# Sums of squares by token quarters on 32 partitions each, root and reciprocal on 128 columns

## The reference

```python
def layer_norm(x, g, b):
    x32 = x.astype(jnp.float32)
    mu = jnp.mean(x32, axis=-1, keepdims=True)
    var = jnp.mean(jnp.square(x32 - mu), axis=-1, keepdims=True)
    y = (x32 - mu) * lax.rsqrt(var + LN_EPS)
    return (y * g.astype(jnp.float32) + b.astype(jnp.float32)).astype(x.dtype)

def rms_norm(x, g):
    x32 = x.astype(jnp.float32)
    y = x32 * lax.rsqrt(jnp.mean(jnp.square(x32), axis=-1, keepdims=True) + RMS_EPS)
    return (y * g.astype(jnp.float32)).astype(x.dtype)
...
    a = jax.nn.silu(layer_norm(a, ln_a_g, ln_a_b))          # branch a, width 512
...
    for i in range(DEPTH):                                   # second block
        h = rmsnorm(x, norm_g[i]) * (1.0 + sc[:, None, :]) + sh[:, None, :]
...
    return rmsnorm(x, norm_f)
```

## Time and profile before

| | |
|---|---|
| Time, median of 3 runs | 2353.86 us |
| Lowest and highest run | 2351.16 and 2355.52 us |
| Profiled execution, span of its instructions (its whole time is not given apart) | 2352.3 us |
| TensorE busy | 2254.0 us, 96% |
| VectorE busy | 1487.5 us, 63% |
| ScalarE busy | 850.4 us, 36% |
| GpSimd busy | 1082.5 us, 46% |
| Mean granted TensorE clock, as a share of 2.4 GHz | 0.988 |

### The profile page before, as it was taken

How to read it: one execution, slowest core, us unless ns; L and a number is a source line. 1 busy time by engine, 2 the same in 40 slices (tenths; PEclk the granted TensorE clock), 3 DMA queues, 4 the chain that set the end, 5 groups by cost and what they waited for, 6 DMA issues and landing times.

```text
span 2352.3 us, 29969 instructions
## 1 busy us (share of the span) xinstructions
PE 2254.0 (96%) x10766; PEld 1834.4 (78%) x10766; DVE 1487.5 (63%) x2357; ACT 850.4 (36%) x1387; POOL 1082.5 (46%) x1273
## 2 busy tenths in 40 slices
PE   6899999999999999999999999999999999999997
PEld 3688777788668877788867888887877878788886
DVE  5989866554478986765368776555775766533322
ACT  2443334222353333422245434344343444433321
POOL 1565436565446543666534455341444344443343
PEclk9999999999999999999999999999999999999999
DMA  8432224664243221354322223233244242222222
GB/s 307 134 110 82 68 73 143 207 202 156 72 143 108 81 67 59 130 169 149 116 81 73 92 99 104 79 116 119 85 123 138 90 126 77 71 72 72 72 81 72
DMA packets 93204, 259.80 MB, mean 110 GB/s; under 512 B 10129, under 2 KB 11537, under 8 KB 92945
## 3 DMA queue, kind: packets, MB, share of 16 engines
q1 hardware_dynamic: 71392, 210.23, 28.6%
q10 hardware_dynamic: 21680, 47.79, 5.7%
HBM read 237.01 MB, written 20.97 MB: 110 GB/s over the span
## 4 chain that ended last, share of the span: by engine, by line
PE 41%; issue 29%; POOL 19%; DVE 7%; ACT 2%; DMA 1%; POOLq 0%; ACTq 0%; DVEq 0%; SPq 0%
POOL t L422 19%; PE bank L2132 13%; PE bank L2133 13%; PE bank L2134 13%; DVE t L1786 3%; PE bank L2206 1%; DVE t L1224 1%; PE bank L2183 1%; DMA t<-blocks 1%; PE bank L2522 1%; DVE t L1228 0%; PE bank L2225 0%; DVE t L1783 0%; POOL t L432 0%; DVE t L1257 0%
## 5 line engine op out<-in xcount | busy, mean ns | idle before, releaser
L422 POOL TENSOR_TENSOR t<-t,t 128x256 fp32r<-128x256 f32 x1208 | 1030.5, 884 | 1179.4 <-ACT t L485 1178.9
L2132 PE MATMUL bank<-t,t 128*128 128x512 f32 (+1 forms) x3056 | 1175.4, 385 | 32.9 <-DVE t L1224 9.4
L2133 PE MATMUL bank<-t,t 128*128 128x512 f32 (+1 forms) x3056 | 1148.4, 376 | 0.0
L2134 PE MATMUL bank<-t,t 128*128 128x512 f32 (+1 forms) x3056 | 1147.2, 375 | 0.0
L2132 PEld LDWEIGHTS bank<-t,t 128*128 128x128 f32 x3056 | 580.0, 190 | 163.5 <-issue 16.0
L2133 PEld LDWEIGHTS bank<-t,t 128*128 128x128 f32 x3056 | 580.0, 190 | 103.2 <-issue 4.2
L2134 PEld LDWEIGHTS bank<-t,t 128*128 128x128 f32 x3056 | 578.4, 189 | 105.1
L485 ACT ACTIVATE t<-t 128x1024 fp32r<-128x1024 f32 x302 | 317.2, 1054 | 287.5 <-PE bank L2134 240.1
L1288 DVE SCALAR_TENSOR_TENSOR t<-t,t,t 128x512 f32<-128x512 f32 x168 | 156.4, 950 | 101.8 <-DMA t<-w_ada 62.0
L1571 DVE SCALAR_TENSOR_TENSOR t<-t,t,t 128x512 f32<-128x512 f32 x240 | 206.1, 859 | 6.7
L1228 DVE SCALAR_TENSOR_TENSOR t<-t,bank 128x512 f32<-128x512 f32 x112 | 76.7, 685 | 153.3 <-ACT t L1181 59.9
(11 more groups left out here) (251 smaller groups left out, 1731.2 us busy)
## 6 DMA issues: line engine op xcount, KB each, us to landing
t<-blocks SPq DMA_DIRECT2D x306, 512.0 KB, 3.6
t<-w_ada SPq DMA_DIRECT2D x144, 256.0 KB, 2.7
t<-w_ada SPq DMA_DIRECT2D x20, 512.0 KB, 11.6
xm_park<-t ACTq DMA_DIRECT2D x16, 384.0 KB, 2.3
s_park<-t ACTq DMA_DIRECT2D x16, 384.0 KB, 2.3
t<-xm_park ACTq DMA_DIRECT2D x16, 384.0 KB, 4.5
t<-s_park ACTq DMA_DIRECT2D x16, 384.0 KB, 5.0
xc_park<-t ACTq DMA_DIRECT2D x16, 256.0 KB, 2.3
```

The lines of the kernel that those rows point to most:

```text
L422: low = pool.tensor_tensor(w_lo[slot][:, part], w_raw[slot][:, part], w_hi[slot][:, part].bitcast(F32), ALU.subtract)
L2132: pe.matmul(out, wh, xh, start=start, stop=False)
L2133: pe.matmul(out, wh, xl, start=False, stop=False)
L2134: return pe.matmul(out, wl, xh, start=False, stop=stop)
```

## The change

The norms named above sum, root and invert in another layout. The 512 tokens are cut into four quarters of 128. For each tile of squares TensorE now issues four products instead of one (`sum_quarters`): each takes 32 columns of ones and 128 tokens, and writes 32 partitions of the bank, quarter j on partitions 32j to 32j + 31. The sums are then 128 x 128, and ScalarE's root and VectorE's reciprocal work on 128 columns. `spread` brings the result back to 128 x 512: four products of 128 columns, whose stationary operand is one column of the identity matrix repeated 128 times, which picks row 32j. It writes a PSUM bank, and VectorE scales the tiles with that bank instead of `tmp[2]`.

TensorE's queue gets the spreads at fixed places, each with a wait for VectorE's reciprocal: in the middle of a chunk (`middle`) for the q norms, for branch a (in `merge(0, 1)`) and for the layer norm of layer 1 (in the first context tile), and between fillers for the other layer norm, `n0` and `n1`, where seven fillers become one, the spread, and two. The last norm's spread ends TensorE's program. The sum of the keys and values' squares waits in addition for the scaled q latents (`qn`), since both use bank 2. The wait of the first context tile for the root `x_std` is gone.

```diff
             def norm_std(cols, n, label, tmp=tmp, bank=3):
                 act.wait_ge(pe_done, P(*label, "sq", n - 1))
+                if cols == S:
+                    cols = S // 4
                 act.activation(tmp[2][:, 0:cols], banks[bank][:, 0:cols], ACT.Sqrt, bias=eps_rms[:], scale=1.0 / (128 * n))\
...
-                act.activation(tmp[2][:], banks[3][:], ACT.Sqrt, bias=eps_x[:], scale=1.0 / D).then_inc(act_done, a(l, "x_std"))
+                act.activation(tmp[2][:, 0:128], banks[3][:, 0:128], ACT.Sqrt, bias=eps_x[:], scale=1.0 / D).then_inc(act_done, a(l, "x_std"))
...
             def norm_recip(cols, label, tmp=tmp):
                 wa(*label, "std")
+                if cols == S:
+                    dve.reciprocal(tmp[2][:, 0:S // 4], tmp[2][:, 0:S // 4]).then_inc(dve_done, d(*label, "rstd"))
+                    wp(*label, "spread")
+                    return
...
             def x_norm(l, j):
-                dve.scalar_tensor_tensor(x[:, j, :], x[:, j, :], V("ln_g", l, j), tmp[2][:], ALU.mult, ALU.mult).then_inc(dve_done, d(l, "x_norm", j))
+                dve.scalar_tensor_tensor(x[:, j, :], x[:, j, :], V("ln_g", l, j), banks[6][:], ALU.mult, ALU.mult).then_inc(dve_done, d(l, "x_norm", j))
...
                 wa(l, "x_std")
-                dve.reciprocal(tmp[2][:], tmp[2][:]).then_inc(dve_done, d())
-                wd()
-                wd()
+                dve.reciprocal(tmp[2][:, 0:128], tmp[2][:, 0:128]).then_inc(dve_done, d(l, "x", "rstd"))
+                wp(l, "x", "spread")
...
+            def sum_quarters(bank, tile, first, last, label):
+
+
+                for j in range(4):
+                    mm = pe.matmul(bank[32 * j:32 * j + 32, 0:128], ones[:, 0:32], tile[:, 128 * j:128 * (j + 1)], start=first, stop=last)
+                mm.then_inc(pe_done, p(*label))
+
+            def spread(bank, quarters, label):
+
+
+                pe.wait_ge(dve_done, Dn(*label, "rstd"))
+                for j in range(4):
+                    row = ident[:, 32 * j:32 * j + 1].to_broadcast([128, 128])
+                    mm = pe.matmul(bank[:, 128 * j:128 * (j + 1)], row, quarters[:, 0:128], start=True, stop=True)
+                mm.then_inc(pe_done, p(*label, "spread"))
...
-                    keep_busy(5, 7)
+                    keep_busy(5, 1)
+                    spread(banks[6], tmp[2], (l - 1, "x"))
+                    keep_busy(5, 2)
...
-                    sum_rows(banks[2], tmp[j % 2][:], 3, j, (l, "q_sq", j))
+                    sum_quarters(banks[2], tmp[j % 2], j == 0, j == 2, (l, "q_sq", j))
                 pe.wait_ge(act_done, A(l, "q_lat", 0))
-                u_chunk(banks[0], B_KVL(l) + 1, (l, "kv_lat", 1))
+                turn = lambda: spread(banks[2], tmp[2], (l, "q"))
+                u_chunk(banks[0], B_KVL(l) + 1, (l, "kv_lat", 1), turn if l else None)
...
-                u_chunk(banks[1], B_KR(l), (l, "k_rope"))
+                u_chunk(banks[1], B_KR(l), (l, "k_rope"), None if l else turn)
...
                     pe.wait_ge(act_done, A(l, "kv_lat_sq", j))
+                    if j == 0:
+                        pe.wait_ge(dve_done, Dn(l, "qn", 2))
...
-                    sum_rows(banks[3], tmp[j % 2][:], NA, j, (l, "a_sq", j))
-                merge(0, 1)
+                    sum_quarters(banks[3], tmp[j % 2], j == 0, j == NA - 1, (l, "a_sq", j))
+                merge(0, 1, lambda: spread(banks[3], tmp[2], (l, "a")))
...
-            pe.wait_ge(act_done, A(L1 - 1, "x_std"))
-            context_tile(0)
+            context_tile(0, lambda: spread(banks[6], tmp[2], (L1 - 1, "x")))
             context_tile(1)
             norm_sums(range(KT), S, ("n0",), sq_t, 5)
-            keep_busy(7, 7)
+            keep_busy(7, 1)
+            spread(banks[5], tmp[2], ("n0",))
+            keep_busy(7, 2)
...
             sums_of_two(("nf",), f_sum, f_s[(KT - 1) % 2])
+            spread(banks[3], f_rstd, ("nf",))
```

More of the change, by code:

```diff
@@ L1754, in _ @@
             norm_recip(S, ("n0",))
-            norm_parts(x, uH, uL, range(KT), S, lambda j: ada[:, 2, j:j + 1], ("n0",), ready=lambda j: (L1 - 1, "y", j))
+            norm_parts(x, uH, uL, range(KT), S, lambda j: ada[:, 2, j:j + 1], ("n0",), ready=lambda j: (L1 - 1, "y", j), rstd=banks[5])
             def xm_parts(h, c):
@@ L2063, in _ @@
             norm_recip(S, ("n1",))
-            norm_parts(x, uH, uL, range(KT), S, lambda j: ada[:, 4, j:j + 1], ("n1",))
+            norm_parts(x, uH, uL, range(KT), S, lambda j: ada[:, 4, j:j + 1], ("n1",), rstd=banks[3])
             def fu_parts(g):
@@ L2138, in w_at, with chunk @@
                 return h[:, s * 128:(s + 1) * 128], lo[:, s * 128:(s + 1) * 128]
-            def chunk(out, tiles, label, ends=()):
+            def chunk(out, tiles, label, ends=(), middle=None):
                 for n, (b, s, xh, xl) in enumerate(tiles):
+                    if n == len(tiles) // 2 and middle:
+                        middle()
                     if n == 0 or b != tiles[n - 1][0]:
@@ L2153, in chunk, with u_chunk @@
                     pair_columns(b)
-            def u_chunk(bank, b, label):
-                chunk(bank[:], [(b, k, uH[:, k, :], uL[:, k, :]) for k in range(KT)], label, (b,))
+            def u_chunk(bank, b, label, middle=None):
+                chunk(bank[:], [(b, k, uH[:, k, :], uL[:, k, :]) for k in range(KT)], label, (b,), middle)
             def first_chunks(out, b, labels, ready, xh=uH, xl=uL, middle=None):
@@ L2218, in context_tile @@
                 for k in range(KT):
+                    if k == KT // 2 and middle:
+                        middle()
                     product(banks[2 + c][:, 0:CTX], *w_at(b, k), cH2[:, k, :], cL2[:, k, :], k == 0, k == KT - 1)
@@ L2223, in norm_sums @@
                     pe.wait_ge(act_done, A(*label, "sq", j))
-                    tile = sq_t[j % 3] if tmp is sq_t else tmp[j % 2]
+                    if tmp is sq_t:
+                        sum_quarters(banks[bank], sq_t[j % 3], j == 0, j == KT - 1, (*label, "sq", j))
+                        continue
+                    tile = tmp[j % 2]
                     pe.matmul(banks[bank][:, 0:cols], ones[:], tile[:, 0:cols], start=(j == 0), stop=(j == KT - 1))\
@@ L2439, in _, with merge @@
                         turn_outputs(3)
-                def merge(jj, k):
+                def merge(jj, k, middle=None):
                     n = 3 * jj + k
@@ L2772, in _ @@
             sums_of_two(("n1",), tmp[3], sq_t[(KT - 1) % 3])
-            keep_busy(7, 7)
+            keep_busy(7, 1)
+            spread(banks[3], tmp[2], ("n1",))
+            keep_busy(7, 2)
             def fu(g):
```

40 lines of the change are left out of this document (19 added, 21 removed).

## The result

The changed kernel took 2341.55 us (median of 4 executions, 2338.44 to 2344.25), beside 2352.99 of the kernel before on the same chip. The ratio is 0.9948 with a 95% interval of 0.9931 to 0.9964. That is 12.2 us less than before by the ratio (11.4 by the medians), where 14.1 less, to 2339.8, were forecast. The mean of the four is 0.9946, or 12.8 us.

The account below looks back on a forecast made before the run. TensorE, busy for 96% of the span, was taken as the bound. Gains of 3.87, 5.5, 4.6 and 3.6 us sum to 17.6; less 3.5 for the clock, 14.1 from 2353.9 gives 2339.8 us, range 2335 to 2349.

Parts of the forecast that it names:

- The fixed part per norm: Every changed norm: shorter reciprocal saves 2.40 us, shorter root 0.33, spread costs 1.15; gain 1.58 us.
- Quarters side by side: Sums on TensorE: four quarter products in different column groups overlap, holding TensorE 0.25 us instead of 0.87.
- rival B: Sums: quarters run one after another, 0.88 us a sum; only 5.7 us gained, 2348.2 us; chance 0.17.
- Rival C: Sums: each change of column group drains TensorE, 1.24 us a sum; slower, 2359.7 us; chance 0.08.
- Place 1: End of layer 0: root starts 2.29 us earlier, and with the fixed 1.58 the gain is 3.87 us.
- Place 2: End of layer 1 and the norm behind it: first scaled tile starts at 1232.85 instead of 1238.34, 5.5 us gained.
- Place 3: Norm before the Fourier layer and the last norm: 2.3 us gained each, together 4.6.
- Branch a: Norm of branch a: shorter sums, and the 1.30 us wait behind it goes; 1.8 us a layer, 3.6 together.
- The q norms: q norms of both layers: shorter sums and the spread's cost, bounded by -0.4 and +0.9 a layer; taken as 0.
- The clock: Sparser TensorE work brings 1.2 GHz stretches; five places at 0.7 take back 3.5 us, bounds 0 and 8.5.
- Rival A: Clock falls over bound work in all five places, taking 8.5 us; 9.1 us gained, 2344.8 us; chance 0.20.
- The sum: Whole kernel: place gains total 17.6 us, less 3.5 for the clock, so 14.1 us gained.

Follow-up runs that it names:

- The mean of the four: Mean over four timed groups of the changed kernel, unedited, each beside the kernel before: ratios 0.9948, 0.9941, 0.9939 and 0.9954.
- e1_one_group: Changed kernel with all quarters after a norm's first sum written to the same 32 partitions, one column group: 2345.62 us, ratio 0.9961.
- e2_warm: Changed kernel plus 192-column, 128-output filler behind sums at both layer ends and the norm behind layer 1, and 512-column filler before two products: 2342.23 us, ratio 0.9954.
- e3_whole: Changed kernel without edit, yardstick of its group: 2340.88 us, ratio 0.9954 to the kernel before.
- e1_q_full: Changed kernel with the q norms of both layers put back to full sums, 512-column root and reciprocal, no spread: 2338.99 us, ratio 0.9936.
- e3_even_warm: As e2_warm, but the filler behind each sum is four side-by-side products with 32 outputs instead of one with 128: 2338.39 us, ratio 0.9939.
- e4_bank_factor: Kernel before with branch a's 512-column reciprocal written to a bank, where the four products behind it read it: 2350.24 us, ratio 0.9991.
- e1_a_full: Changed kernel with branch a's norm put back in both layers: full sums, 512-column root and reciprocal, no spread: 2346.67 us, ratio 0.9972.
- the four executions: Profiled executions of the unedited changed kernel, one from each of its four timed groups; they won 9.8, 18.3, 16.8 and 16.0 us.
- the first execution: Profiled execution of the changed kernel from its first measurement: span 2342.5 us, 9.8 us won.

## Why the prediction was right, and where its terms were not

- *The fixed part per norm, 1.58 us*: right. Reciprocals took 0.95 and roots 0.37 (0.34 to 0.37), the spread 1.16 at full clock (2326.25 above), as worked out.
- *Quarters side by side, 0.25 us a sum*: right. The timeline of the changed kernel has two sums that lay ready in one row, and three in another:

```profile
371.86 0.65 PE L2217 MATMUL bank<-t,t 128*32 128x128 f32 x16
...
1223.11 0.86 PE L2217 MATMUL bank<-t,t 128*32 128x128 f32 x24
```

  One takes 0.43, two 0.65, three 0.86, so a sum holds TensorE for 0.22; e1_one_group gives 0.87 for rival B's form. Rival B is refuted. Sums in a row are thus 0.87 / 0.22 = 4.0 times as fast. A single sum, from its first start to its last end, takes 0.43 against about 1.08 (0.87 and the 0.21 that the last end adds), 2.5 times. The Trainium skill gives a factor of 2.38 for three groups ("TensorE: Matmul & The Clock Gate", Part 3). For the time that a sum holds TensorE the measured 4.0 goes first.
- *Rival C, a drain at a change of column group*: refuted, since positions change at no cost. A change of the form does cost, 0.34 us for a pair of changes in e2_warm. The Trainium skill's rule ("TensorEngine Tiling (Array Packing)", Key Properties), that changing the mode drains and changing the tile doesn't, agrees on both counts.
- *Place 1, 3.87 us*: right at full clock and a little small. With the clock up it gave 4.6 in three kernels (e3_whole, e1_q_full, e3_even_warm). Of that 0.5 comes from one `x_norm` product (L1384), which took 1.23 us before, beside GpSimd, and 0.74 with the factor in a bank. The rest is the squares' pace, 0.60 instead of the 0.635 of the forecast.
- *Place 2, 5.5 us*: right at full clock (5.2 and 5.0), 2.6 to 3.7 in the executions where it fell.
- *Place 3, 2.3 each*: 1.9 and 2.2 at full clock. In the norm before the Fourier layer the root starts 0.85 us behind the last square instead of 0.48, since ScalarE makes a high part of weights (L485) from 1995.75 for 1.04 us.
- *Branch a, 1.8 a layer*: mis-sized in layer 0, 3.6 to 4.8. The failed step is "so I charge nothing, with a gain of 0.1 each as the other bound": where GpSimd works beside VectorE the gain is 0.54 an operation, and e4_bank_factor wins 1.5 us in layer 0 by that alone (1.4 in layer 1, but there e1_a_full wins 1.4 without it). The wait before the first y product did go, but it goes in e4_bank_factor and, in layer 1, in e1_a_full as well; it hangs on VectorE's and the queue's timing as a whole, not on the spread.
- *The q norms, 0*: below the lower bound of -0.4 in most executions, about -1 us in layer 0, and 0 in layer 1. I had looked for VectorE's wait in the chain, but not for where in TensorE's order the spread stands. It is 0.7 us behind the reciprocal at full clock, where layer 0 won 0.3 to 0.4, and 2.1 or more where half clock had made TensorE late.
- *The clock, 3.5 us*: the right size, and the term that decides between executions. Against their full-clock values (4.6, 5.2, 1.9 and 2.2) the four executions fall short at places 1, 2 and 3 by 4.8, 3.7, 1.3 and 3.1 us, 3.2 in the mean. The term had spread its 3.5 us over five places, and the q norm's loss comes on top. Rival A, a loss of 8.5 over all places, was not reached; the first execution came nearest.
- *The sum*: the places of the table won 14.6 to 18.6, 16.7 in the mean, beside 17.6 less 3.5, 14.1, forecast. A gain at branch a that was 2.4 larger than forecast made up for the start and the q norm (-2.8 in the mean), which were forecast at 0, and the stretches between the places added 1.4, forecast at 0 too. That the sum comes so near the forecast is in this part luck. Of those -2.8 about 1 us is the q norm. The kernels with the old q norm also lie 0.3 to 2.0 us behind at 343 (4.9 in e4_bank_factor), which is how the start varies.

Not settled: why e1_a_full loses 7.3 us in time while its trace accounts for 3.5 to 4.7 at branch a. Its trace lost another 3.6 us between 1630 and 1650, in the mLSTM layer, with the clock at half from 1628.1 to 1634.9; the four executions of the changed kernel lie between 0.4 lost and 0.4 won there. Whether the clock falls there in most executions, and whether branch a has to do with it, one profile can't tell. Nor did I time the filler without the sums of place 2, so the share of each fall in the time is read from traces only.

## What to carry to other kernels

Sums over partitions by a matrix of ones need only 32 output columns: cut the free axis in four and place the quarters in four column groups, and TensorE's time falls to a quarter. The reciprocal went from 3.35 to 0.95 us and the root from 0.69 to 0.37; the spread, 1.16, is the price. When that makes TensorE idle, look at the granted clock behind it. If you fill, take products of the same form as their neighbours, and reckon with what the filler costs at half clock, since a fall came in spite of it. Look up for each VectorE operation whether GpSimd runs beside it; a second operand in a bank can be worth more than the operation that was shortened.

## What the runs showed of the hardware that was not expected

- Two float32 inputs in SBUF beside a working GpSimd: 1.22 us for 128x512 instead of 0.68 with one input in a bank, and GpSimd slower by half too.
- A product with 128 outputs behind ones with 32: 0.14 us lost, and 0.20 on the way back; among products with 32 outputs in four positions nothing is lost.
- The same program differs by 8.5 us between profiled executions, in large part because half clock is granted at other moments: the same spread took 1.16 us in one and 2.07 in another.
